# Retention's attention ahead of its gate blocks, single-pass gather and scatter in the expert loop, pairs of experts in two layouts

## The chip, the cores and the metric

The kernel runs on one core of a Trainium2 chip. The metric is the device time of one execution in microseconds (us). Of each version several executions are timed, and the medians are compared. A separate execution is profiled by the hardware; the rows and durations below come from that one.

## What is computed

Two networks run one after the other on 256 tokens of width 1024, all in float32. The first (modulated layers with attention, a Fourier mixer and dense MLPs) is not touched. The second has two layers: each is a mixer followed by a mixture of experts. The mixer of layer 0 is an attention with forget gates ("fox"), that of layer 1 is retention.

```
retention:  q, k, v, gate = split(h @ w_in)                # 1024 -> 6 blocks of 1024 columns: q, k, v0, v1, g0, g1
            q, k = rotary(q), rotary(k) / 16
            o = ((q @ k.T) * decay) @ v                    # 4 heads, 256 tokens
            o = (o - mean(o)) * rsqrt(var(o) + eps) * gn_gain
            y = (silu(gate) * o) @ w_out                   # 2048 -> 1024
experts:    32 experts in 4 groups; each token takes the best group and 2 experts in it
            y[t] = sum over its 2 experts e of gate[t, e] * (silu(x_t @ w_g[e]) * (x_t @ w_u[e])) @ w_down[e]
```

Every expert's weights (w_gu 1024 x 1024, w_down 512 x 1024) are read once a layer.

## The kernel before

Everything is written by hand, engine by engine, with semaphores; the order of the work on an engine is the order of the code. Activations lie transposed (feature on the partition, token on the free axis). SP issues nearly all the loads.

**Dense weights.** A matrix is cut in blocks of 1024 columns, and a block in 4 chunks of 256 rows (1 MB). `dense_w` is a ring of 4 chunks. SP loads a chunk (L461) when PE has done with the one 4 earlier; ACT makes its high part (`w_high`, L428) and DVE the rest (`w_low`, L435), both in the type fp32r, which PE multiplies in one pass. `by_rows` goes through a block chunk by chunk: 8 output tiles, 2 rows of tiles in a chunk, and 3 matmuls for each (high weights x high input, low x high, high x low; L552 to L554). So a block has 192 matmuls of 256 columns. A matmul on plain float32 is one instruction in the code but two records (and two weight loads) in the profile.

**Retention.** PE: blocks q, k, v0, v1, g0, g1 of `ret_in`; the scores of 4 heads (L1058); times v (`ret_pv`, L1070, L1071); the mean over a head's 512 features as a matmul with a constant (`gn_mean`, L582); the variance (`gn_var`); then `keep_warm` (L595), 16 matmuls with constants whose result nobody reads; then the two blocks of `ret_out`. ACT takes the silu of g0 and g1 as they leave PE (L1104), and the square root of the variances (L1116). DVE multiplies scores with the decay (L2207), subtracts the mean (L2212), multiplies gate, value and gain (L2219), and then for each head takes the reciprocal (L1530), multiplies it in (L2226), waits for ACT's high part of the result (L1499) and makes the low one (L1555); only then may PE start a chunk of `ret_out`. `ret_out` has two slots for its high parts (`w_high_ret`), so ACT may split a chunk when PE has done with the one two earlier. On SP, once g1 is done, the 8 loads of the first 4 pieces of the next expert pair come ahead of `ret_out`'s last 4 chunks.

**Experts.** `experts(l)` first turns h into tokens on the partitions (L879), normalises (L1405 on ACT, L1963 on DVE: `hn_tok`), and computes the logits (L886); DVE chooses groups and experts, counts, and gives each row of an expert a place (L1953 to L2087). Then come 16 pairs of experts in a hardware loop. The two experts of a pair share one pass of 128 rows. Per pair PE does: `project` (L945): 8 row tiles x 2 halves, moving the 1024 x 1024 weights of both experts past the gathered rows in column tiles of the array that work at the same time; `gather` (L929) for the next pair: 16 float32 matmuls of 128 columns that pick 128 rows out of `hn_tok` by a 0/1 matrix `pick`; `turn_hidden` (L970), `turn_pick` (L965); `add_up` (L976): 8 float32 matmuls of 256 columns that add the previous pair's output `y_sb` to 4 banks through the transposed weighted matrix `pick_wT`; and `down` (L957). ACT copies the left half of y out of its bank (L1430), DVE the right half (L2102); PE's `pending` waits for both ahead of the next `gather`. The 128 rows are divided 64/64 between the two experts, or 32/96 or 96/32 where both fit that way; three variants of `project` and `down` stand in the code, chosen by a register (L1022, L1038). Where an expert has more rows than its share, a further round is run for the pair.

The weights of a pair are 12 pieces of 1 MB: `load_experts(l, pair, j)` issues two DMAs (L470), one for each expert, j = 0 to 3 for w_gu and 4, 5 for w_down. There is one buffer for each piece: SP issues piece j of the next pair when PE has done with piece j of this one.

## Time and profile before

| | before |
|---|---|
| median of 3 runs | 2210.24 us (2209.28 to 2216.31) |
| the profiled execution's own time | 2208.49 us |
| its span in the profile | 2206.7 us |
| PE busy | 2080.8 us (94%) |
| PE weight loads busy | 1519.7 us (69%) |
| DVE busy | 884.1 us (40%) |
| ACT busy | 687.7 us (31%) |
| moved by DMA | 603.25 MB, mean 273 GB/s |
| PE's share of the chain that ended last | 85% |

The two expert loops run from 953.5 us to 1431.5 us and from 1704.8 us to 2183.0 us of the span; retention lies between 1437 and 1680 us. An engine's busy share is a mean over stages that have different limits; a busy PE is not a PE at its peak, since matmuls overlap. The chain is followed back from the last instruction to whatever released it.

### The profile page before, as it was taken

Reading aid. Unit: us, or ns where it says so; the run is one execution under the profiler, and the core shown is the slowest. Engines: PE = TensorE matmul, PEld = TensorE weight load, DVE = VectorE, ACT = ScalarE, POOL = GpSimd, SP = SyncE. Lnnn points to the kernel's source line nnn. Section 1 sums busy time; section 2 is a strip of 40 time slices with the busy share of each in tenths; the row PEclk is TensorE's granted clock in tenths of the full one; section 3 lists DMA queues with packets and bytes.
Section 4 is the critical chain, followed back from the end, with each engine's and each line's share of the span. In section 5 each row is a group of like instructions: output and inputs, shape, how many; then the busy total and the mean of one; then the engine's idle time right before and its main releaser. Section 6 shows DMA issues by size and latency. Waiting matters only on the chain.

```text
span 2206.7 us, 37943 instructions
## 1 busy us (share of the span) xinstructions
PE 2080.8 (94%) x15688; PEld 1519.7 (69%) x15689; DVE 884.1 (40%) x1459; ACT 687.7 (31%) x1070; POOL 80.3 (4%) x119
## 2 busy tenths in 40 slices
PE   7997899998999998889999999989998999999998
PEld 5876899988999898744544444588987444444454
DVE  5866677755643544521111111156366111111112
ACT  3434455253553456511111111144342111111111
POOL 0110111101000200000000000000000000000000
PEclk9998999999999999989999999989998999999999
DMA  9731388912654251689999999625642899999992
GB/s 360 266 128 39 118 306 320 333 42 77 249 190 175 78 189 39 255 330 422 421 422 422 421 422 422 267 90 189 214 189 98 366 421 421 422 422 422 422 422 123
DMA packets 108115, 603.25 MB, mean 273 GB/s; under 512 B 10078, under 2 KB 10532, under 8 KB 58868
## 3 DMA queue, kind: packets, MB, share of 16 engines
q1 hardware_dynamic: 95872, 559.39, 64.0%
q0 software_dynamic: 11872, 42.35, 5.2%
q8 instruction: 74, 1.21, 0.2%
q14 instruction: 21, 0.17, 0.0%
q10 hardware_dynamic: 276, 0.13, 0.0%
HBM read 600.74 MB, written 1.05 MB: 273 GB/s over the span
## 4 chain that ended last, share of the span: by engine, by line
PE 85%; DVE 5%; ACT 4%; DMA 3%; issue 3%; SPq 0%; DVEq 0%; ACTq 0%
PE bank L945 20%; PE bank L957 10%; PE bank L552 10%; PE bank L553 9%; PE bank L554 9%; PE bank L929 6%; PE bank L976 5%; PE bank L582 4%; DMA dense_w<-in_w_in 1%; PE bank L562 1%; PE bank L563 1%; PE bank L561 1%; PE bank L632 1%; DMA dense_w<-in_mlp_w 1%; ACT w_high L428 1%
## 5 line engine op out<-in xcount | busy, mean ns | idle before, releaser
L945 PE MATMUL bank<-expert_w,work 128*32 128x512 f32 (+1 forms) x4032 | 446.1, 593 | 19.1 <-issue 19.1
L945 PEld LDWEIGHTS bank<-expert_w,work 128*32 128x32 f32 (+1 forms) x4032 | 156.7, 110 | 307.0 <-issue 307.0
L435 DVE TENSOR_TENSOR w_low<-dense_w,w_high 128x2048 fp32r<-128x2048 f32 x112 | 256.1, 2290 | 223.5 <-ACT w_high L428 222.9
L428 ACT ACTIVATE w_high<-dense_w 128x2048 fp32r<-128x2048 f32 x120 | 228.6, 1911 | 313.4 <-DMA dense_w<-in_mlp_w 197.6
L957 PE MATMUL bank<-expert_w,work 128*32 128x512 f32 (+1 forms) x2016 | 226.4, 594 | 0.0
L2092 DVE TENSOR_TENSOR work<-work,bank 128x512 f32<-128x512 f32 x32 | 22.0, 688 | 391.4 <-ACT work L1419 391.4
L929 PEld LDWEIGHTS bank<-work 128*128 128x128 f32 x1088 | 137.3, 205 | 43.9 <-issue 43.9
L957 PEld LDWEIGHTS bank<-expert_w,work 128*32 128x32 f32 (+1 forms) x2016 | 63.6, 110 | 144.4 <-issue 144.4
L929 PE MATMUL bank<-work 128*128 128x128 f32 x1088 | 143.7, 293 | 13.9 <-issue 7.7
L552 PE MATMUL bank<-u_pairs_mlp,w_high 128*128 128x256 f32 x512 | 146.1, 285 | 7.3 <-ACT u_pairs_mlp L1144 5.9
L553 PE MATMUL bank<-u_pairs_mlp,w_low 128*128 128x256 f32 x512 | 145.6, 284 | 0.0
L554 PE MATMUL bank<-u_pairs_mlp,w_high 128*128 128x256 f32 x512 | 145.6, 284 | 0.0
L553 PE MATMUL bank<-hidden_pairs,w_low 128*128 128x256 f32 x512 | 145.1, 283 | 0.0
L554 PE MATMUL bank<-hidden_pairs,w_high 128*128 128x256 f32 x512 | 145.1, 283 | 0.0
L552 PE MATMUL bank<-hidden_pairs,w_high 128*128 128x256 f32 x512 | 145.1, 283 | 0.0
L1419 ACT ACTIVATE work<-bank 128x512 f32<-128x512 f32 x32 | 19.1, 597 | 392.3 <-PE bank L945 392.3
L552 PE MATMUL bank<-u_pairs,w_high 128*128 128x256 f32 x448 | 130.1, 290 | 9.0 <-DVE u_pairs L1537 5.3
L553 PE MATMUL bank<-u_pairs,w_low 128*128 128x256 f32 x448 | 129.0, 288 | 0.0
L554 PE MATMUL bank<-u_pairs,w_high 128*128 128x256 f32 x448 | 128.9, 288 | 0.0
L976 PE MATMUL bank<-work 128*128 128x256 f32 x544 | 123.2, 380 | 1.7 <-ACT work L1430 1.7
L1430 ACT ACTIVATE work<-bank 128x512 f32<-128x512 f32 x32 | 19.1, 597 | 323.5 <-PE bank L957 323.5
L976 PEld LDWEIGHTS bank<-work 128*128 128x128 f32 x544 | 100.8, 190 | 15.7 <-ACT work L1430 3.5
(387 smaller groups left out, 3610.3 us busy)
## 6 DMA issues: line engine op xcount, KB each, us to landing
expert_w<-in_expert_w_gu SPq DMA_DIRECT2D x256, 1024.0 KB, 13.5
expert_w<-in_expert_w_down SPq DMA_DIRECT2D x128, 1024.0 KB, 9.8
dense_w<-in_mlp_w SPq DMA_DIRECT2D x64, 1024.0 KB, 5.3
dense_w<-in_ret_w_in SPq DMA_DIRECT2D x24, 1024.0 KB, 5.3
u<-in_ada_w POOLq DMA_DIRECT2D x40, 512.0 KB, 6.0
work<-in_ada_w POOLq DMA_DIRECT2D x40, 512.0 KB, 7.0
dense_w<-in_fox_w_in SPq DMA_DIRECT2D x16, 1024.0 KB, 5.1
dense_w<-in_w_in SPq DMA_DIRECT2D x12, 1024.0 KB, 7.9
```

Source lines behind the costliest of these rows:

```text
L428: nc.scalar.activation(HIGH_OF[at], dense_w[:, at % RING], ACT.Copy, scale=scale).then_inc(S("w_high_ready"), 1)
L435: ins = nc.vector.tensor_tensor(w_low[:, at % RING], dense_w[:, at % RING], high, ALU.subtract)
L552: mm(out[:, 0:SEQ], w[:, c], high[:, k, :], start=start, stop=False)
L553: mm(out[:, 0:SEQ], w_rest[:, c], high[:, k, :], start=False, stop=False)
L554: return mm(out[:, 0:SEQ], w[:, c], low[:, k, :], start=False, stop=stop)
L561: mm(out[:, :], high[:, k, rows], w[:, c], start=start, stop=False)
L562: mm(out[:, :], high[:, k, rows], w_rest[:, c], start=False, stop=False)
L582: last = mm(bank(t)[:, 0:SEQ], weights, src[:, k, :], start=k == 0, stop=k == tiles - 1)
L929: last = mm(free[2 + half][:, (k % 4) * P:(k % 4 + 1) * P], every_other(hn_tok[:, tt], k), source[:, tt, :], start=tt == 0, stop=tt == TT - 1)
L945: last = mm(free[half][cols, :], rows[:, k, cols], pieces[:, k // 2, a, k % 2, half * 512:(half + 1) * 512], start=k == 0, stop=k == KT - 1)
L957: last = mm(free[2 + half][cols, :], hidT[:, f, cols], pieces[:, (KT + f) // 2, a, f % 2, half * 512:(half + 1) * 512], start=f == 0, stop ...
L976: last = mm(total[k // 2][:, (k % 2) * SEQ:(k % 2 + 1) * SEQ], y_sb[:, k * P:(k + 1) * P], pick_wT.rearrange("p t n -> p (t n)"), start=Fa ...
```

## The change

It has four parts.

1. **Pairs.** The divisions are now 64/64, or 96 rows for the crowded expert and 32 for the other (`LARGE`). Where the second expert of a pair is the crowded one, SP loads the pair swapped: it reads a 0/1 from `more_i` at the head of each turn (a new wait for `more_known` ahead of the loop) and adds it to the address. Pair 0, which is loaded before the counts are known, is not swapped. Of the three variants of `project` and `down` two remain. DVE's arithmetic on the counts is rewritten.
2. **Gather and scatter.** `hn_tok` and `y_sb` become a high and a low part each in fp32r. `gather` has 32 single-pass matmuls of 128 columns in place of 16 float32 ones, `add_up` 16 single-pass ones of 256 columns in place of 8. The matrix for `add_up` is now 0/1 (`pickT`), and the weight of a row is multiplied into y. ACT makes the whole high part (two instructions), DVE the whole low part (two instructions, each after ACT's). The same holds for `hn`: ACT makes 4 high quarters, DVE 4 low ones.
3. **Retention.** PE does scores, values, means and variances right after v1, then g0 and g1, then `ret_out`; `keep_warm` is gone. DVE multiplies gain and reciprocal deviation into the values ahead of the gates. On SP the decay's load moves ahead of 20 loads of `ret_in`, and the loads of the next pair's pieces stand between `ret_out`'s last 4.
4. **A small load.** The gains of the expert norm (8 KB, on POOL's queue) are loaded after 56 of the modulation loads that it stood ahead of.

The core of the diff:

```
@@ TILES
-  ("ret_v1", 4), ("ret_g0", 8), ("ret_g1", 8), ("ret_scores", 4), ("ret_pv", 8), ("gn_mean", 4), ("gn_var", 4),
+  ("ret_v1", 4), ("ret_scores", 4), ("ret_pv", 8), ("gn_mean", 4), ("gn_var", 4), ("ret_g0", 8), ("ret_g1", 8),
@@ SP
+                sp.wait_ge(S(f"more_known_{l}"), 1)
                 with sp.Fori(1, PAIRS) as i:
+                    swap = sp.value_load(more_i[0:1, ds(i + 3 * PAIRS, 1)], min_val=0, max_val=1)
                     for j in range(PIECES // 2):
                         sp.wait_ge(expert_used, PIECES * (PAIRS * l + i - 1) + 2 * j + 2)
-                        load_experts(l, i, j)
+                        load_experts(l, i, j, swap)
...
                     wait_tile(sp, TILES["ret_g1"] + 7)
-                    for j in range(4):
-                        load_experts(1, 0, j)
                     for j in range(RING):
                         load(chunk("ret_out", 1, j))
+                        load_experts(1, 0, j)
@@ PE, experts
                     for k in range(4 * half, 4 * half + 4):
                         for tt in range(TT):
-                            last = mm(free[2 + half][:, (k % 4) * P:(k % 4 + 1) * P], every_other(hn_tok[:, tt], k),
-                                      source[:, tt, :], start=tt == 0, stop=tt == TT - 1)
+                            for x in (hn_high, hn_low):
+                                last = mm(free[2 + half][:, (k % 4) * P:(k % 4 + 1) * P], x[:, tt, k * P:(k + 1) * P], source[:, tt, :],
+                                          start=tt == 0 and x is hn_high, stop=tt == TT - 1 and x is hn_low)
...
                     for k in range(KT):
-                        last = mm(total[k // 2][:, (k % 2) * SEQ:(k % 2 + 1) * SEQ], y_sb[:, k * P:(k + 1) * P],
-                                  pick_wT.rearrange("p t n -> p (t n)"), start=False, stop=False)
+                        for y in (y_high, y_low):
+                            last = mm(total[k // 2][:, (k % 2) * SEQ:(k % 2 + 1) * SEQ], y[:, k * P:(k + 1) * P], pickT,
+                                      start=False, stop=False)
...
-                    for first in SHARES:
+                    for first in (SLOTS, LARGE):
                         with pe.If(first_rows == first):
                             project(xg, loaded, expert_used, first)
@@ PE, retention
-            for i, name in enumerate(("ret_q", "ret_k", "ret_v0", "ret_v1", "ret_g0", "ret_g1")):
+            for i, name in enumerate(("ret_q", "ret_k", "ret_v0", "ret_v1")):
...
-            keep_warm(TILES["ret_out"], 2 * WARM)
+            for i, name in ((4, "ret_g0"), (5, "ret_g1")):
+                by_rows("ret_in", i, TILES[name], 8, columns(*second))
@@ ACT, experts
-                for q in (0, 2):
-                    t = TILES[f"hn_{l}"] + q
-                    evac(fn(hn_tok[:, 0, q // 2 * 512:(q // 2 + 1) * 512], bank(t)[:, :], ACT.Copy, scale=small[:, 88:89]), t)
-                fn(y_sb[:, 0:512], const[:, 0:512], ACT.Copy, scale=0.0).then_inc(S("y_act"), 1)
+                for q in range(4):
+                    fn(hn_part(hn_high, q), bank(TILES[f"hn_{l}"] + q)[:, :], ACT.Copy, scale=small[:, 88 + q % 2:89 + q % 2]).then_inc(S("hn_high"), 1)
...
                 def take_y(done):
-                    fn(y_sb[:, 0:512], free[2][:, :], ACT.Copy).then_inc(done, 1)
+                    for half in range(2):
+                        fn(y_high[:, half * 512:(half + 1) * 512], free[2 + half][:, :], ACT.Copy, scale=slot_w).then_inc(done, 1)
@@ DVE, experts
-                V.memset(y_sb[:, 512:1024], 0.0).then_inc(S("y_dve"), 1)
-                V.memset(pick_wT, 0.0).then_inc(S("pick_wT_ready"), 1)
+                V.tensor_scalar(y_low, const[:, 0:D], 0.0, None, ALU.mult).then_inc(S("y_dve"), 1)
+                V.tensor_scalar(pickT, const[:, 0:SEQ], 0.0, None, ALU.mult).then_inc(S("pick_wT_ready"), 1)
...
+                def low_of_hn(q):
+                    dve.wait_ge(S("hn_high"), 4 * l + q + 1)
+                    evac(V.scalar_tensor_tensor(hn_part(hn_low, q), bank(TILES[f"hn_{l}"] + q)[:, :], small[:, 88 + q % 2:89 + q % 2],
+                                                hn_part(hn_high.bitcast(f32), q), ALU.mult, ALU.subtract), TILES[f"hn_{l}"] + q)
...
                 def take_pick_wT(done):
-                    V.tensor_copy(pick_wT, free[1][:, 0:SEQ].rearrange("p (t n) -> p t n", t=TT)).then_inc(done, 1)
+                    V.tensor_reduce(slot_w, free[1][:, 0:SEQ], AX.X, ALU.add)
+                    V.tensor_scalar(pickT, free[1][:, 0:SEQ], 0.0, None, ALU.is_gt).then_inc(done, 1)
+
+                def take_y(made, at, done):
+                    for half in range(2):
+                        dve.wait_ge(made, at + half + 1)
+                        eight = slice(half * 512, (half + 1) * 512)
+                        last = V.scalar_tensor_tensor(y_low[:, eight], free[2 + half][:, :], slot_w, y_high[:, eight].bitcast(f32),
+                                                      ALU.mult, ALU.subtract)
+                    last.then_inc(done, 1)
@@ DVE, retention
+                inv_std(gn_rstd[:, hd, :], TILES["gn_var"] + hd)
                 for n in range(4 * hd, 4 * hd + 4):
-                    wait_evac(dve, TILES[f"ret_g{n // 8}"] + n % 8)
-                    V.scalar_tensor_tensor(rgate[:, n, :], ro[:, n, :], vcol(VEC1["gn"] + n), rgate[:, n, :],
-                                           ALU.mult, ALU.mult).then_inc(S("ret_gated"), 1)
+                    V.scalar_tensor_tensor(ro[:, n, :], ro[:, n, :], vcol(VEC1["gn"] + n), gn_rstd[:, hd, :],
+                                           ALU.mult, ALU.mult).then_inc(S("ret_scaled"), 1)
```

How the change moves instructions is seen at three places. The first is PE between `project` and `down` in the expert loop (`work` holds the gathered-from tokens, the pick matrices and y). Before:

```order
L1025 REGISTER_ALU
L929 MATMUL bank<-work 128x128 x16
L970 MATMUL bank<-const,work 128x128 x4
L965 MATMUL bank<-const,work 128x128 x2
L976 MATMUL bank<-work 128x256 x8
```

With the change (the first two rows stand 16 times over, as do the last two for 8 row tiles):

```order
L940 MATMUL bank<-pick,hn_high 128x128
L940 MATMUL bank<-pick,hn_low 128x128
L978 MATMUL bank<-const,work 128x128 x4
L973 MATMUL bank<-const,work 128x128 x2
L985 MATMUL bank<-pickT,y_high 128x256
L985 MATMUL bank<-pickT,y_low 128x256
```

The place of the four steps is the same; gather and scatter have twice the instructions, each of a single pass.

The second is DVE from the scores of retention to the residual add after `ret_out`, where PE waits for it. Before:

```order
L2207 TENSOR_TENSOR work<-bank,work 128x384 x4
L2212 TENSOR_TENSOR work<-work,bank 128x1024 x4
L435 TENSOR_TENSOR w_low<-dense_w,w_high_ret 128x2048
L2219 SCALAR_TENSOR_TENSOR work<-work,vec 128x256 x16
L435 TENSOR_TENSOR w_low<-dense_w,w_high_ret 128x2048
L1530 RECIPROCAL work<-work 128x256
L2226 TENSOR_TENSOR work<-work 128x1024
L1555 TENSOR_TENSOR rgate_low<-work,rgate_high 128x256 x4
L1530 RECIPROCAL work<-work 128x256
L2226 TENSOR_TENSOR work<-work 128x1024
L1555 TENSOR_TENSOR rgate_low<-work,rgate_high 128x256 x4
L435 TENSOR_TENSOR w_low<-dense_w,w_high_ret 128x2048 x2
```

With the change (L438 is the low part of a chunk, `w_high` without _ret that of a gate block; L2260 multiplies a gate with its values):

```order
L2251 SCALAR_TENSOR_TENSOR work<-work,vec 128x256 x4
L438 TENSOR_TENSOR w_low<-dense_w,w_high 128x2048 x3
L2260 TENSOR_TENSOR work<-work 128x1024 x2
L438 TENSOR_TENSOR w_low<-dense_w,w_high 128x2048
L1582 TENSOR_TENSOR rgate_low<-work,rgate_high 128x256 x8
L438 TENSOR_TENSOR w_low<-dense_w,w_high_ret 128x2048 x2
L2260 TENSOR_TENSOR work<-work 128x1024 x2
L1582 TENSOR_TENSOR rgate_low<-work,rgate_high 128x256 x8
L438 TENSOR_TENSOR w_low<-dense_w,w_high_ret 128x2048 x6
L1973 TENSOR_TENSOR h<-h,bank 128x256 x8
```

The reciprocals and the gain now stand ahead of the gate blocks' splits, and between a gate block and `ret_out` only one multiplication for a head and the low parts are left.

The third is SP between the two expert loops. Before:

```order
L461 DMA dense_w<-in_ret_w_in 128x2x1024 x20
L509 DMA work<-in_decay 128x1536
L461 DMA dense_w<-in_ret_w_out 128x2x1024 x4
L470 DMA expert_w<-in_expert_w_gu 128x2048 x8
L461 DMA dense_w<-in_ret_w_out 128x2x1024 x4
L470 DMA expert_w<-in_expert_w_down 128x2048 x4
```

With the change (the `ret_out` chunk and the two expert loads behind it stand three times):

```order
L516 DMA work<-in_decay 128x1536
L468 DMA dense_w<-in_ret_w_in 128x2x1024 x20
L468 DMA dense_w<-in_ret_w_out 128x2x1024 x5
L478 DMA expert_w<-in_expert_w_gu 128x2048 x2
L468 DMA dense_w<-in_ret_w_out 128x2x1024
L478 DMA expert_w<-in_expert_w_gu 128x2048 x2
L478 DMA expert_w<-in_expert_w_down 128x2048 x4
```

Each of the last chunks of `ret_out` but the first has the two loads of an expert piece ahead of it.

## Rows read from the trace of the kernel before

**Rows 1.** The page's slices: busy tenths of PE and DMA, each slice 55 us
```profile
PE   7997899998999998889999999989998999999998
...
DMA  9731388912654251689999999625642899999992
```

**Rows 2.** Window over layer 1's expert loop: length, busy by engine, clock, DMA share, GB/s
```profile
1740.00:2160.00 420.00, 412.69 (x3504) 202.55 (x3500) 73.54 (x217) 60.27 (x113) 0.00 (x0) 1.00 1.01 422
```

**Rows 3.** Chain of waits, expert loops: start us, us, what
```profile
1225.58 13.96 PE bank L945 x64
...
1402.39 13.94 PE bank L945 x128
...
1718.72 3.67 issue
...
2124.26 13.94 PE bank L945 x128
2138.20 3.97 PE bank L929 x32
2142.86 3.46 PE bank L976 x16
...
2153.83 13.94 PE bank L945 x128
...
2182.95 0.61 ACT work L1430
2183.74 3.69 PE bank L976 x16
```

**Rows 4.** Line L470, piece 3 of pair 2, layer 1: issue and landing
```profile
L470 SPq DMA_DIRECT2D expert_w<-in_expert_w_gu x2: 332/332/333, 1753.9 to 1754.4; - x2
...
DMA to landing us min/median/max: 12.9/13.8/14.8
```

**Rows 5.** The same of pair 15, layer 1
```profile
L470 SPq DMA_DIRECT2D expert_w<-in_expert_w_gu x2: 333/333/333, 2138.4 to 2138.9; - x2
...
DMA to landing us min/median/max: 16.3/17.3/18.3
```

**Rows 6.** The same of pair 15, layer 0
```profile
L470 SPq DMA_DIRECT2D expert_w<-in_expert_w_gu x2: 332/332/333, 1387.0 to 1387.5; - x2
...
DMA to landing us min/median/max: 17.2/18.2/19.1
```

**Rows 7.** SP's timeline: the first loads of pair 1's w_down, layer 1
```profile
1735.79 4.28 SPq L470 DMA_DIRECT2D expert_w<-in_expert_w_down  x4
```

**Rows 8.** Windows: block g1, keep_warm, behind it, ret_out's start, layer 1's first gather
```profile
1622.30:1629.40 7.10, 7.08 (x33) 5.90 (x31) 7.07 (x11) 0.47 (x1) 0.00 (x0) 1.00 0.00 0
1629.40:1631.80 2.40, 0.00 (x0) 0.01 (x1) 1.92 (x4) 1.29 (x4) 0.00 (x0) 1.00 0.00 0
1631.80:1637.00 5.20, 5.18 (x43) 5.20 (x44) 4.68 (x8) 1.39 (x5) 0.00 (x0) 1.00 0.00 0
...
1697.00:1703.20 6.20, 6.13 (x32) 5.95 (x32) 1.72 (x11) 2.31 (x5) 0.00 (x0) 0.62 0.02 4
...
1570.00:1592.90 22.90, 22.90 (x193) 22.90 (x192) 4.59 (x2) 6.71 (x10) 0.00 (x0) 1.00 0.60 219
```

**Rows 9.** PE's timeline in ret_out: the wait in brackets
```profile
1656.38 0.39 PE L552 MATMUL bank<-rgate_high,w_high_ret 128*128 128x256 f32 x1 [1.29 <-DVE w_low L435]
```

**Rows 10.** DVE's timeline ahead of layer 1's logits
```profile
1683.71 1.41 DVE L1963 TENSOR_SCALAR work<-bank,small 128x512 f32<-128x512 f32 x2
```

**Rows 11.** The page's groups and issues: splits of a chunk, DVE on a bank, a chunk's load
```profile
L435 DVE TENSOR_TENSOR w_low<-dense_w,w_high 128x2048 fp32r<-128x2048 f32 x112 | 256.1, 2290 | 223.5 <-ACT w_high L428 222.9
...
L2092 DVE TENSOR_TENSOR work<-work,bank 128x512 f32<-128x512 f32 x32 | 22.0, 688 | 391.4 <-ACT work L1419 391.4
...
dense_w<-in_ret_w_in SPq DMA_DIRECT2D x24, 1024.0 KB, 5.3
```

**Rows 12.** Chain of waits: float32 records of 256 columns while the clock is low
```profile
1439.69 6.70 PE bank L582 x16
```

247 lines of the change are left out of this document (139 added, 108 removed).

## The prediction, made before the changed kernel ran

> **What bounds the kernel now.** The page's slices come first: PE is busy nearly everywhere, and in the two expert loops the DMA engines are full as well [rows 1]. A window over layer 1's loop says it sharply: DMA share 1.01 at 422 GB/s for 420 us, PE busy 413 of 420 at full clock, ACT and DVE mostly idle [rows 2]. Two full resources need a third view, the chain of waits. It shows a pair of experts as PE's work alone: project 13.94 us, gather 3.97, add_up 3.46, then down; and from one project to the next 2153.83 - 2124.26 = 29.57 us [rows 3]. No step waits for a load. But a pair's 12 MB are 12.58 million bytes, and at 422 GB/s they take 29.8 us, 0.26 us longer than PE. So the loads must lose ground, and the landings show it: piece 3 of pair 2 in layer 1 landed 14.8 us after its issue, at 1754.4 + 14.8 = 1769.2 [rows 4]; that of pair 15 took 18.3 us and landed at 2157.2 [rows 5]. PE first needs piece 3 three quarters into project, 10.46 us after its start: at 2164.3 for pair 15. It had 7.1 us to spare. In layer 0 it landed at 1387.5 + 19.1 = 1406.6 and was needed at 1402.39 + 10.46 = 1412.85: 6.2 us to spare [rows 3, 6]. **PE bounds the loops, with DMA just below it**: a faster PE wins about that reserve once a layer, and no more.
>
> Retention is PE's alone, with three losses: 7.1 us of matmuls with constants, 2.4 us of idleness behind them, while DVE and ACT finish the first head, and 1.29 us in ret_out [rows 8, 9].
>
> **Expert loops.** add_up has 16 single-pass matmuls of 256 columns in place of 16 float32 records. In block g1 such matmuls follow each other every 22.9 / 193 = 0.119 us [rows 8], so it takes 1.9 us in place of 3.46: 1.5 less. gather has 32 single-pass matmuls of 128 columns, a form that the trace does not show. From below: half the price of the 256-column form, 0.06 us, 1.9 us in all. From above: the price of a float32 record of 256 columns, 3.46 / 16 = 0.216 us, 6.9 us in all. The nearest rows agree with each other: float32 records of 128 columns come every 3.97 / 32 = 0.124 us, single-pass ones of 256 every 0.119 [rows 3, 8], and both load 128 x 128 weights for each matmul, which fills PEld in g1 (22.90 of 22.90 us). I take 0.119, 3.8 us in all, 0.1 less than before. PE's pair becomes 28.0 us, less than the 29.8 of its loads.
>
> The Trainium skill's page TensorE: Matmul & The Clock Gate (Back-to-back issue gap) gives about 81 ns for a matmul of 128 columns in a stream with its weight loads. By that estimate gather would take 2.6 us; the sum would be some 5 us lower, from the first and last pair of each layer, since between them the loads bound. No row here shows it.
>
> So the reserve is used up at 1.9 us a pair: by about pair 7 PE waits for piece 3, some 1.8 us each time. What moves the end: SP issues pair 1's first w_down piece when pair 0 has used its own, at 1735.79 in layer 1 [rows 7], and from there on DMA never rests. A shorter pair 0 brings this and all later landings forward by 1.6 us. Piece 3 of pair 15 lands at 2157.2 - 1.6 = 2155.6; the last quarter of project is 3.5 us; from there to the end of down were 2182.95 - 2153.83 - 13.94 = 15.2 us and are 13.6 [rows 3]. The loop ends at 2172.7 in place of 2182.95: **-10.2 us**. Layer 0 in the same way: 1406.6 - 1.6 + 3.5 = 1408.5 in place of 1416.3, and 1.6 behind it: **-9.4 us**. The 3.67 us of issue after pair 0's first project [rows 3] I leave as it is; with other code it may be 0 or double, which moves each layer by up to 4 us either way.
>
> Would waits of 1.8 us lower the clock? Behind the warming PE idled 2.40 us, and the granted clock stayed 1.00 in the windows on both sides [rows 8]. I charge nothing.
>
> Behind the loop, y's chain was 0.79 us from the last matmul to add_up. Now ACT makes one half (0.61), DVE its low part (0.69, as on another whole bank), ACT's second half lies beside this, and DVE's second follows: with hand-offs 2.2 us, 1.4 more; add_up saves 1.7 of its 3.69 [rows 3, 11]. **-0.3 a layer.** Inside the loop the same chain, and one more DVE pass over the pick matrix, have 13.9 us of project as their cover. Without it the chain would cost its 2.2 us a pair.
>
> **Pairs and variants.** The pair with two tiles of 64 columns took 13.96 us for project, those with four of 32 took 13.94 [rows 3]: fewer instructions, no time. Worked out from the reference's inputs, pair 0 holds 1 and 4 rows in layer 0 and 10 and 7 in layer 1, and every crowded expert (at most 78 rows) shares with one of at most 29 or counts under 65, so no pair gets a further round; one would cost a whole pass, near 29 us. SP's register read lies between w_down's issues and the next expert_used, and SP's queue has a reserve of microseconds there: nothing. Its new wait ahead of the loop ends before PE's first project, which frees the first piece.
>
> **Routing.** ACT's first high quarter (0.61) now precedes DVE's two low ones (2 x 0.69) where both engines worked at once for 1.41 [rows 10, 11]: +0.8. Zeroing 1024 elements by arithmetic in place of a MEMSET of 512 adds 0.3 (bounds: nothing, and the 0.7 of another instruction on 512). The two later low quarters fall in DVE's wait for PE's counts; the counts' own chain is two or three small steps shorter, -0.2. **+0.9 a layer.** The first gather is as slow as before (6.13 us for 32 records at a mean clock of 0.62).
>
> **Retention.** The six blocks and the statistics keep their length; ret_out follows g1 directly. Gone are 7.1 + 2.4 + 1.3: **-10.8 us**. The cover: values' statistics, reciprocals and gains are DVE work under g0's 23 us; g0's silu, product and parts lie under g1; g1's lie under ret_out's first block. If that cover fails, the first product, high and low part cost some 5 us. The last chunks of ret_out now queue behind 2 MB of expert weights: 2.1 million bytes at 422 GB/s are 5.0 us, then 5.3 for the chunk, somewhat less than DVE on ACT (say 1.9), and 2.3 on DVE, together 14.5, against three chunks of 5.7 (22.9 / 4) that PE has in between [rows 8, 11]. The decay's load waits ahead of loads that could not start anyway. The 8 KB load saves or costs nothing that a wait shows.
>
> **Sum.** -10.8 - 10.2 - 9.4 - 0.6 + 1.8 = -29.2 us. The profiled execution took 2208.5 us, so 2179.3; the median of the runs is 1.7 higher, so **2181 us**. A measurement of this kernel tells from no change what exceeds 0.3%, 6.6 us.
>
> **Rivals.**
> - *Gather turns slow (slower).* If a single-pass matmul of only 128 columns costs as much as a float32 record of 256, gather takes 6.9 us, a pair 29.57 + 2.9 - 1.5 = 31.0: PE bounds again, 16 x 1.4 = 22 us more a layer. At the low clock of the first gather such records take 6.70 / 16 = 0.42 us [rows 12], so that one takes 13.4 in place of 6.1. Together 59 - 0.6 - 10.8 + 1.8 = +50: 2260 us. It decides from 0.18 us a matmul, where the loops lose what retention gains. For it: the form is nowhere in the trace. Against it: no form that is there is bound by anything but columns and weight loads. 0.16.
> - *Retention wins nothing.* The removed idleness comes back as waits for splits or evacuations, since ACT splits two gate chunks ahead of the values' evacuation: 2192 us. The arithmetic above speaks against it. 0.10.
> - *The loops win little*: waits for loads cost clock or restart the queue late, so that the 20 us fall away: 2201 us. Rows 8 speak against the clock, and six pieces in flight against a dry queue. 0.08.
> - *Loads run faster.* Now PE bounds the loops, and perhaps 422 GB/s is its pace and not DMA's. Then 16 x 1.6 a layer are won, 2150 us. The growing landing times contradict it [rows 4, 5]. 0.04. The Trainium skill's page DMA: Bandwidth & Descriptors (Where 436 GB/s comes from) puts the fabric's ceiling at 435 GB/s, an estimate of 28.9 us a pair, which would give most of this; the trace's 422 stands against it.
>
> **Numbers.** The forecast has the other 0.62. Its own bounds are 2172 (gather at its lower price, 1.9 us less in the first and last pair of each layer, and a shorter stall) to 2192. Taking in the second and third rival the range is 2172 to 2204, which leaves out 0.20. Faster: 0.62 + 0.10 + 0.04 + 0.03 of the third rival = 0.79; within 0.3%: 0.05; slower: 0.16.
>
> **What would show it.** In the changed profile: PE from v1 to ret_out without a gap, no constant matmuls; pairs about 29.8 us apart in the later half of each loop, at DMA share 1.01, with waits before the last quarter of project whose releaser is the expert load; the first pairs 28.0 us apart; gather near 3.8 and add_up near 1.9 us. A gather over 5.8 us, or pairs over 30 us apart, would make the prediction wrong; so would loops with no wait for a load.

## The result, and the profile after

| | before | after |
|---|---|---|
| median of the runs shown | 2209.76 us (4 runs, 2200.74 to 2216.31) | 2230.72 us (4 runs, 2224.55 to 2235.49) |
| ratio, 95% interval | | 1.0096 [1.0049, 1.0143] |
| the profiled execution | 2208.49, span 2206.7 | 2224.55, span 2222.7 |

The change made the kernel 1% slower, about 21 us; forecast were 2181 us and a range that ended at 2204. The stretches of the two profiled executions say where (a loop runs from the first `project` of a layer to its last `down`):

| | before | after | difference | forecast |
|---|---|---|---|---|
| start of layer 0's loop | 953.5 | 949.3 | -4.2 | +0.9 |
| loop of layer 0 | 478.0 | 523.1 | **+45.1** | -9.4 |
| between the loops (with retention) | 273.3 | 263.3 | -10.0 | -10.2 |
| loop of layer 1 | 478.1 | 465.0 | -13.1 | -10.2 |
| behind it | 23.8 | 22.1 | -1.7 | -0.3 |

Three of the five came out within 3 us of the forecast. The start of layer 0's loop is 5 us off, which is at least in part scatter (late_gains, below). One is off by 55 us, and in one layer only. The page of the changed kernel shows the place in its slices, which answer to [rows 1] (each slice is 55.6 us):

```profile
PE   7997899998999998899999999989999999999997
...
DMA  9731389803645251789998957935447699999994
GB/s 347 268 133 40 141 305 331 316 35 114 229 177 184 78 189 52 292 367 422 422 422 369 374 227 295 422 128 171 133 142 313 258 422 422 422 422 422 422 422 206
```

PE looks busy as before, but in layer 0's loop (slices 18 to 27) DMA falls from 422 to 227 GB/s; in layer 1's it doesn't. The chain of waits in layer 0 has the cause, in three pairs of 16 (8, 10 and 11, counted from 0):

```profile
1167.49 7.02 PE bank L965 x32
1174.51 31.61 PE bank L953 x96
1206.12 3.72 PE bank L940 x32
...
1210.61 1.91 PE bank L985 x16
1212.52 15.88 PE bank L965 x48
1228.39 13.88 PE bank L953 x64
```

x64 is a pair in two tiles of 64 columns, x96 one of the new division 96/32 in three tiles, of 64, 32 and 32 columns. Its `project` takes 31.6 us and not 13.9, its `down` 15.9 and not 7.0: 26.7 us more. PE's weight loads in the same `project` say how (columns: start, time, and in brackets the idle time before):

```profile
1181.25 0.14 PEld L953 LDWEIGHTS bank<-expert_w,work 128*32 128x32 f32 x4 [0.81 <-issue]
1182.23 0.19 PEld L953 LDWEIGHTS bank<-expert_w,work 128*64 128x64 f32 x2 [0.84 <-issue]
1183.23 0.14 PEld L953 LDWEIGHTS bank<-expert_w,work 128*32 128x32 f32 x4 [0.81 <-issue]
```

The 64-column tile and the two 32-column ones take turns, 0.99 us each; two tiles of one width share 0.86 us (13.73 / 16). The three tiles cost two turns where four equal tiles cost one.

Layer 1 has no 96/32 pair, and there the forecast can be read step by step. Its chain, which answers to [rows 3]:

```profile
1735.60 16.63 PE bank L953 x64
1752.23 3.72 PE bank L940 x32
...
1756.72 1.90 PE bank L985 x16
...
1765.64 13.73 PE bank L953 x64
...
1792.79 13.73 PE bank L953 x64
...
2128.24 25.34 DMA expert_w<-in_expert_w_gu
2153.59 0.14 issue
2153.72 3.67 PE bank L953 x16
...
2158.06 25.35 DMA expert_w<-in_expert_w_gu
2183.42 0.14 issue
2183.55 3.65 PE bank L953 x16
```

Gather takes 3.72 us (forecast 3.8) and add_up 1.9 (1.9). Behind pair 0 the pairs are 27.1 us apart at first (1792.79 - 1765.64; forecast 28.0); from pair 6 on they are 29.83 apart (2183.42 - 2153.59), and the last quarter of `project` (x16) is released by the load of piece 3, as forecast. PE's busy time in the window that answers to [rows 2] fell from 412.7 to 399.1 us:

```profile
1740.00:2160.00 420.00, 399.08 (x2180) 191.99 (x2177) 87.39 (x239) 69.74 (x130) 0.00 (x0) 1.00 1.00 418
```

Retention: windows over g0's and g1's end, then `ret_out`, which answer to [rows 8, 9], show PE without a gap:

```profile
1618.04:1664.00 45.96, 45.96 (x385) 45.96 (x385) 29.43 (x32) 20.82 (x31) 0.00 (x0) 1.00 0.48 161
1664.00:1710.18 46.18, 46.18 (x387) 46.18 (x387) 20.70 (x22) 15.94 (x17) 0.00 (x0) 1.00 0.74 296
```

### The profile page after: what moved, and what is told of

It is laid out like the page before. It is cut to its first block, busy times and chain, and to the rows that moved or that the text cites. A ratio compares the mean times of both kernels' runs of the same rounds, so it can differ in the third digit from the quotient of the medians.

```text
span 2222.7 us, 32423 instructions
## 1 busy us (share of the span) xinstructions
PE 2093.5 (94%) x12824; PEld 1473.4 (66%) x12825; DVE 919.7 (41%) x1529; ACT 713.5 (32%) x1108; POOL 80.5 (4%) x119
## 4 chain that ended last, share of the span: by engine, by line
PE 72%; DMA 17%; DVE 4%; ACT 4%; issue 2%; SPq 0%; ACTq 0%; DVEq 0%
PE bank L953 16%; DMA expert_w<-in_expert_w_gu 16%; PE bank L561 10%; PE bank L562 10%; PE bank L563 10%; PE bank L965 7%; PE bank L591 4%; PE bank L940 4%; PE bank L985 2%; PE bank L571 1%; PE bank L570 1%; PE bank L572 1%; PE bank L641 1%; DMA dense_w<-in_w_in 1%; DVE work L1557 1%
## 5 line engine op out<-in xcount | busy, mean ns | idle before, releaser
L953 PE MATMUL bank<-expert_w,work 128*64 128x512 f32 (+1 forms) x2144 | 508.8, 600 | 31.9 <-DMA expert_w<-in_expert_w_gu 28.3
L953 PEld LDWEIGHTS bank<-expert_w,work 128*64 128x64 f32 (+1 forms) x2144 | 154.1, 135 | 380.4 <-issue 380.4
L438 DVE TENSOR_TENSOR w_low<-dense_w,w_high 128x2048 fp32r<-128x2048 f32 x112 | 256.0, 2290 | 213.3 <-ACT w_high L431 212.5
L965 PE MATMUL bank<-expert_w,work 128*64 128x512 f32 (+1 forms) x1072 | 253.4, 597 | 0.0
L965 PEld LDWEIGHTS bank<-expert_w,work 128*64 128x64 f32 (+1 forms) x1072 | 72.1, 134 | 157.3 <-issue 153.0
L1429 ACT ACTIVATE work<-bank 128x512 f32<-128x512 f32 x32 | 19.1, 598 | 457.9 <-PE bank L953 457.9
L2133 DVE SCALAR_TENSOR_TENSOR y_low<-bank,small,y_high 128x512 fp32r<-128x512 f32 x64 | 45.1, 746 | 252.9 <-ACT y_high L1441 252.9
L1441 ACT ACTIVATE y_high<-bank,small 128x512 fp32r<-128x512 f32 x64 | 40.6, 685 | 302.9 <-PE bank L965 302.9
L940 PE MATMUL bank<-pick,hn_high 128*128 128x128 f32 x544 | 128.3, 282 | 4.1 <-DVE pick L2090 4.1
L940 PEld LDWEIGHTS bank<-pick,hn_high 128*128 128x128 f32 x544 | 106.7, 196 | 33.1 <-issue 33.1
L940 PE MATMUL bank<-pick,hn_low 128*128 128x128 f32 x544 | 126.9, 280 | 0.0
```

What stands on the lines that cost most here:

```text
L438: ins = nc.vector.tensor_tensor(w_low[:, at % RING], dense_w[:, at % RING], high, ALU.subtract)
L940: last = mm(free[2 + half][:, (k % 4) * P:(k % 4 + 1) * P], x[:, tt, k * P:(k + 1) * P], source[:, tt, :], start=tt == 0 and x is hn_high, ...
L953: last = mm(free[half][cols, :], rows[:, k, cols], pieces[:, k // 2, a, k % 2, half * 512:(half + 1) * 512], start=k == 0, stop=k == KT - 1)
L965: last = mm(free[2 + half][cols, :], hidT[:, f, cols], pieces[:, (KT + f) // 2, a, f % 2, half * 512:(half + 1) * 512], start=f == 0, stop ...
L1441: fn(y_high[:, half * 512:(half + 1) * 512], free[2 + half][:, :], ACT.Copy, scale=slot_w).then_inc(done, 1)
L2133: last = V.scalar_tensor_tensor(y_low[:, eight], free[2 + half][:, :], slot_w, y_high[:, eight].bitcast(f32), ALU.mult, ALU.subtract)
```

## The experiments

Each ratio is to the kernel before, run on the same chip in the same rounds. Widths are in columns.

### Is it the widths of the tiles?

**four_tiles.** The changed kernel, one line changed:

```
-                            LARGE: [(slice(0, SLOTS), 0), (slice(SLOTS, LARGE), 0), (slice(LARGE, P), 1)]}
+                            LARGE: [(slice(at, at + UNIT), int(at >= LARGE)) for at in range(0, P, UNIT)]}
```

> The changed kernel with the 96/32 division as four tiles of 32 columns, as the kernel before had it. Theory (a tile of 64 columns does not work at the same time as tiles of 32): project of the three 96/32 pairs falls from 31.6 to 13.9 us and down from 15.9 to 7.0; waits for loads of about 2 us a pair appear instead, as in layer 1; the loop of layer 0 falls from 523 to about 465 us, and the kernel's median from 2231 to about 2172 (2165 to 2180), 1.5% or more below the kernel before. Rival (the swapped address makes these pairs' loads or the reading of their weights slow): project of these pairs stays at 31.6 and the time at 2231. Rival (the second variant's code is fetched slowly): project stays well above 20 us.

Measured: 2175.39 us, ratio 0.9841 [0.982, 0.9862]. The loops take 465.0 and 465.1 us. The three pairs wait for their loads like the others. Its chain:

```profile
1188.91 3.68 PE bank L953 x32
1193.25 25.37 DMA expert_w<-in_expert_w_gu
1218.75 3.67 PE bank L953 x16
```

x32 is the last quarter of a 96/32 pair in four tiles, x16 that of a 64/64 pair. The window over these pairs is full of loads again:

```profile
1255.00:1363.00 108.00, 100.83 (x675) 49.14 (x675) 24.09 (x67) 18.14 (x33) 0.00 (x0) 1.00 1.01 422
```

One line is worth 55 us (2230.7 to 2175.4; the spans differ by 53.7). The swapped address and the choice between two variants still stand in this kernel, so they are not the cause, and it is faster than the kernel before and the changed one.

**grouped.** Three tiles again; within each k both matmuls of the 64-column tile come first:

```
+                    return [(half, tile) for wide in (True, False) for half in range(2) for tile in tiles_of[first]
+                            if (tile[0] == slice(0, SLOTS)) == wide]
```

> Still tiles of 64, 32 and 32 columns, but for each row tile the two matmuls of the 64-column tile (left and right half) stand together, and then the four of the 32-column tiles: two changes of width for a row tile in place of four. Theory, with a price of 0.13 us for each change of width (0.988 us for a stretch of one width in place of 0.855): project 8 x (4 x 0.855 + 2 x 0.13) = 29.4 us in place of 31.6, down 14.7 in place of 15.9; kernel about 2222. Rival (no price for the change, each matmul of such a set is only slow): both stay at 31.6 and 15.9, kernel 2231.

Measured (one execution): `project` 29.46 us, `down` 14.81, kernel 2213 us, its loop in layer 0 513.7 us in place of 523.1. Its weight loads:

```profile
1180.88 0.14 PEld L959 LDWEIGHTS bank<-expert_w,work 128*64 128x64 f32 x1 [0.29 <-issue]
1181.31 0.14 PEld L959 LDWEIGHTS bank<-expert_w,work 128*64 128x64 f32 x1 [0.29 <-issue]
1182.26 0.14 PEld L959 LDWEIGHTS bank<-expert_w,work 128*32 128x32 f32 x4 [0.81 <-issue]
1182.72 0.12 PEld L959 LDWEIGHTS bank<-expert_w,work 128*32 128x32 f32 x2 [0.31 <-issue]
```

While the width stays, the next weights are loaded 0.29 us after the last ones (0.31 for 32 columns), beside the running matmul. Where it changes, they wait 0.81 us, until the matmuls in the array have all but ended: the last one began at 1181.74 and is given 0.59 us, the load starts at 1182.26. So there are two prices: tiles of unlike width share no time (0.855 us a matmul), and a change of width costs 0.13 us on top. The first is most of it.

**wide_between.** The order of the three tiles is 32, 64, 32:

```
-                            LARGE: [(slice(0, SLOTS), 0), (slice(SLOTS, LARGE), 0), (slice(LARGE, P), 1)]}
+                            LARGE: [(slice(SLOTS, LARGE), 0), (slice(0, SLOTS), 0), (slice(LARGE, P), 1)]}
```

> The same three tiles, but the 64-column one stands between the two of 32, so that no two tiles of one width follow each other in a set. Theory (only neighbours of equal width work at the same time): of a set and the next, 32, 64, 32 and again 32, 64, 32: the last 32 and the first 32 of the next set are of one width but the latter uses other columns, so they may pair up; then a set costs 0.988 x 2 as before and project stays at 31.6 us. If both go one after the other, a set costs about 2.8 us and project about 45, down 22.7, kernel about 2290. Rival (a set with unequal widths costs what it does by its widths, whatever the order): 31.6.

Measured (one execution): 2228 us.

```profile
1174.62 32.73 PE bank L953 x96
...
1213.74 16.85 PE bank L965 x48
```

It is one turn more than 31.61, 1.1 us: the last 32-column tile of a set pairs up with the first of the next, and only the first and the last of all stand alone. What counts is whether neighbours in the stream have one width, not how a set is made up.

**before_three.** The kernel before, with the three tiles alone:

```
-                    return [(slice(at, at + UNIT), int(at >= first)) for at in range(0, P, UNIT)]
+                    if first > SLOTS:
+                        return [(slice(0, SLOTS), 0), (slice(SLOTS, first), 0), (slice(first, P), 1)]
+                    return [(slice(0, UNIT), 0), (slice(UNIT, SLOTS), 1), (slice(SLOTS, P), 1)]
```

> The kernel before, with nothing of the change but the tiles: wherever it divides 96/32 or 32/96, tiles of 64, 32 and 32 columns take the place of four of 32. It does so in 15 of 16 pairs of layer 0 and, by its trace, in all pairs seen of layer 1. Theory: project 31.6 in place of 13.9 and down 15.9 in place of 7.0 in each, some 26.6 us a pair less the nothing that loads gave, so about 31 x 26.6 = 820 us more: 3030 us. Rival (the cost belongs to the swap, the second variant or another part of the change): 2210 us.

Measured (one execution): 3007 us, 796 more. Without any other part of the change:

```profile
1008.90 31.76 PE bank L947 x96
...
1048.77 15.88 PE bank L959 x48
```

### Where do the loops win?

With this out of the way, each loop gains 13 us. The forecast gave such a gain to the single passes.

**no_add_up.** Left out: the sum of 15 of 16 pairs of each layer.

```
-                    add_up().then_inc(S("added"), 1)
+                    mm(total[0][:, 0:SEQ], y_high[:, 0:P], pickT, start=False, stop=False).then_inc(S("added"), 1)
```

> The kernel with four tiles, where one matmul stands in the loop for the sixteen that add a pair's output: 15 of 16 pairs of a layer are left out of the sum. Theory (the loads bound the loops): PE has 1.8 us less a pair, only the first and the last pair of each layer give it back, 4 x 1.8 = 7 us: 2168; pairs late in the loop still 29.8 us apart. Rival (PE and its waits bound, the loads follow): 32 x 1.8 = 57 us less, 2118.

Measured: 2162.6 us, ratio 0.9785 [0.9752, 0.9819], 12.8 below four_tiles where 7 were expected, and far from 57. In layer 1 pairs start 26.1 us apart and from pair 5 on 29.8: the loads bound the loop. By the profiles its loops are only 0.1 and 2.1 us shorter. The profiled execution is the slowest of its four and four_tiles' the fastest of its five; the rest of the 12.8 I can't place.

**float_gather.** four_tiles, with gather and add_up in float32 again:

```
-                            for x in (hn_high, hn_low):
-                                last = mm(free[2 + half][:, (k % 4) * P:(k % 4 + 1) * P], x[:, tt, k * P:(k + 1) * P], source[:, tt, :],
-                                          start=tt == 0 and x is hn_high, stop=tt == TT - 1 and x is hn_low)
+                            last = mm(free[2 + half][:, (k % 4) * P:(k % 4 + 1) * P], hn_high.bitcast(f32)[:, tt, k * P:(k + 1) * P],
+                                      source.bitcast(f32)[:, tt, :], start=tt == 0, stop=tt == TT - 1)
```

> The kernel with four tiles, with the tokens and y kept whole in float32 and gather and add_up as 16 and 8 float32 matmuls again, as before the change; the low parts are still made but not read. Theory (the prediction's term for the single passes: they bring PE's pair from 29.6 to 28 us, and the loads keep what is beyond 0.26 us a pair): gather 3.97 and add_up 3.46 us return, a pair takes 29.6 us of PE and 29.8 of loads, no wait for a load is left but near the end, and each loop is longer by what pair 0, the last pair and the used-up reserve are worth, 9 to 10 us: 2194. Rival (a loop bound by loads takes what its loads take, whatever PE does): within 3 us of the kernel with four tiles.

**four_again** is four_tiles on the same chip.

> The kernel with four tiles once more, beside the next two on one chip, so that they can be compared with it directly. By its first runs 0.984 of the kernel before, 2175 us.

Measured: 2175.03 us for float_gather, ratio 0.9858 [0.983, 0.9885], against 2172.15 us, 0.9835 [0.9809, 0.9861]. The rival holds: 3 us by the medians and 5 by the ratios, whose intervals overlap, in place of some 20. Its pairs in layer 1:

```profile
1706.55 13.73 PE bank L952 x64
1720.29 3.77 PE bank L939 x32
...
1724.75 3.46 PE bank L983 x16
1728.20 7.02 PE bank L964 x32
1735.22 13.73 PE bank L952 x64
```

A pair takes 28.67 us and not the 29.6 that I expected. 0.2 us of this is gather: its 32 float32 records take 3.77 us where they took 3.97 before, and they do so with four tiles too (float_all_four, below), so the tiles are not the reason. It now reads its weights from adjacent columns and no longer from every other one; that this is the reason no run shows by itself. The rest, 0.7 us, lies almost all between `down` and the next `project`: no idle time is left there, where four 32-column tiles before had 0.5, and the first matmuls of `project` begin before the last of `down` have ended. From its start to gather's `project` itself takes 13.83 us against 13.87. Fifteen times 0.9 is 13 us, twice the reserve of 7. So the loads bind these loops too, if later (from pair 10 on).

**all_four_tiles** and **float_all_four.** four_tiles and float_gather, with 64/64 in four tiles too:

```
-                tiles_of = {SLOTS: [(slice(0, SLOTS), 0), (slice(SLOTS, P), 1)],
+                tiles_of = {SLOTS: [(slice(at, at + UNIT), int(at >= SLOTS)) for at in range(0, P, UNIT)],
```

> The kernel with four tiles, where the 64/64 division too has four tiles of 32 columns in place of two of 64, as most pairs of the kernel before had; single-pass gather and add_up stay. Theory (a pair of two 64-column tiles is 0.2 us shorter in project and has none of the 0.5 us between down and the next project, and either this or the single passes alone is enough to use up the reserve of the loads): pairs of 27.9 us until the loads bind, each loop still about 465 us, kernel within 3 us of the one with four tiles only for 96/32 (2172 to 2175). Rival (the tiles are what shortened the loops): loops of 476 to 478 us, about 2195.

> Both at once: float32 gather and add_up, and four tiles of 32 columns for every division. Theory: the pair is 29.6 us as before the change, nothing uses up the reserve, each loop is 10 to 12 us longer again (475 to 478 us), the kernel 2193 to 2198. Rival (what is saved comes from the number of variants, or from pair 0 alone): loops of 466 to 470 us, 2175 to 2180.

Measured, with ratio to the kernel before, early pairs and loops:

| gather, add_up | 64/64 in | median us | ratio | early pairs us | loop 0, loop 1 us |
|---|---|---|---|---|---|
| single passes | two tiles | 2172.15 | 0.9835 | 27.1 | 470.1, 464.7 |
| float32 | two tiles | 2175.03 | 0.9858 | 28.7 | 467.8, 465.8 |
| single passes | four tiles | 2181.84 | 0.9882 | 27.6 | 464.1, 473.2 |
| float32 | four tiles | 2196.24 | 0.994 | 29.1 | 467.6, 475.9 |

The first two rows ran side by side on one chip, the last two on another. Against the last row, by the ratios, the single passes alone win 0.0058 (12.8 us), the tiles alone 0.0082 (18.1), both together 0.0105 (23.2) and not 30.9. Each ratio is uncertain by 0.002 to 0.003, so that this shortfall alone shows little. My two expectations missed in part: all_four_tiles is 10 us above four_again, not 3, and float_all_four's first loop did not return to 475.

Where the differences lie is seen when the loops of the profiled executions are divided at the second `project` (all in us, layer 0 and layer 1):

| | idle ahead of the first project | first pair | other 15 pairs |
|---|---|---|---|
| kernel before | 1.8, 1.6 | 35.3, 35.0 | 442.6, 443.1 |
| single passes, two tiles | 1.8, 1.7 | 34.6, 29.2 | 435.6, 435.5 |
| float32, two tiles | 1.8, 1.8 | 31.0, 28.7 | 436.8, 437.0 |
| single passes, four tiles | 5.3, 4.9 | 29.9, 38.5 | 434.1, 434.8 |
| float32, four tiles | 5.7, 4.6 | 31.2, 39.0 | 436.4, 437.0 |

Behind the first pair the four are within 3 us of each other, and each is 6 to 9 us below the kernel before. Even the last, which has neither the single passes nor the wide tiles, wins 6.2 us a layer there: its pairs start 29.1 us apart and not 29.6, since gather takes 3.77 us in place of 3.97 and the idle time behind `down` is shorter:

```profile
1361.70 0.24 issue
1361.95 13.94 PE bank L952 x128
```

Between `down` and the next `project` PE idles 0.24 us where the kernel before, with its three variants, idled 0.50. In layer 0 the first pair adds 4.1 us to this (35.3 to 31.2), which brings that loop to 467.6. Fifteen times the 0.46 by which the pairs are nearer are 6.9 us, about the whole reserve, and the last two `project`s of layer 1 already take 14.1 and 14.2 us in place of 13.9. So what is common to all four kernels nearly uses the reserve up; the single passes add 1 to 2 us behind the first pair, the tiles nothing.

The tiles' 18 us are elsewhere. Of the 21.9 us between the spans of the two float32 kernels 10.2 are the first pair of layer 1, and 4.0 and 2.9 are idle time ahead of the two first `project`s. That pair in all_four_tiles' timeline of PE:

```profile
1684.62 1.92 PE L953 MATMUL bank<-expert_w,work 128*32 128x512 f32 x5 [4.91 <-issue]
1687.53 15.86 PE L953 MATMUL bank<-expert_w,work 128*32 128x512 f32 x123 [0.99 <-issue]
1706.09 0.30 PE L940 MATMUL bank<-pick,hn_high 128*128 128x128 f32 x1 [2.70 <-issue]
```

It lasts 38.5 us. Ahead of it and within it lie 4.9 + 1.0 + 2.7 us in which PE waits for nothing that the profile shows, and behind the 2.7 the granted clock fell: from 1706.0 to 1715.5 its mean was 0.64, and gather and add_up took 5.8 and 3.6 us from start to start in place of 4.3 and 2.1.

First pairs also differ between executions of one kernel: in layer 0 that of four_tiles took 31.0 us and that of four_again 34.6, since the clock fell in the second behind 2.5 us of idle time (0.50 from 970 to 975 us) and not in the first behind 1.9.

### What is the idle time in the first pair?

**three_variants.** four_tiles, with a third variant that no pair takes:

```
-                    for first in (SLOTS, LARGE):
+                    for first in (UNIT, SLOTS, LARGE):
```

> The kernel with four tiles, and with the third variant of project and down (32/96) back in the code, where no pair takes it. Theory (the idle time of PE behind the first project of a layer, 4.04 and 3.67 us before and 1.91 and 0 now, is fetching of the code that stands between): it grows back to about 4 us in both layers, pair 0 is that much longer, and the loops, bound by loads that start with pair 0, end about 2 to 4 us later each: 2179 to 2183 against 2175.4. Rival (the gap comes from something else, and code that is not run costs nothing): 2175.4.

Measured: 2182.15 us, ratio 0.9885 [0.9857, 0.9912], 7 us above four_tiles by the medians, 10 by the ratios. The place is not the one that I named: the gap grew ahead of the first project, where the variant that is skipped stands.

```profile
1680.87 7.79 issue
```

In four_tiles it was 1.73 us there; in layer 0, 5.19 against 1.76. Together that is 9.5 us of the 9.3 between the two profiled executions, and the loops themselves are as long as in four_tiles (464.8 and 464.9 us). In all_four_tiles too, where these gaps are 5.3 and 4.9 us, there is more code to skip ahead of the first project: the further round, which no pair takes, has four tiles there. The profile's DMA queue of instructions points the same way (packets, MB, share):

```profile
q8 instruction: 74, 1.21, 0.2%
```

It has 74 packets here and in the kernel before, 73 in the two runs with four tiles for both divisions, 71 and 70 in four_tiles and four_again, 70 in the changed kernel, and 80 in retention_only, below.

The Trainium skill's page Runtime: NRT & Kernel Launch (Terms) says that each engine's instruction memory is refilled in blocks of 16 KB; 1.21 MB in 74 packets is 16.4 KB each, which agrees. That PE waited for such a block in the gaps is argued from this and from the places of the gaps; no row names a releaser.

The idle time between `down` and the next `project` follows the number of variants too: between two 96/32 pairs it was 0.23 us in four_tiles and 0.63 here, like the 0.24 of float_all_four and the 0.50 of the kernel before.

### Retention and the small load

**retention_only.** The kernel before, with part 3 of the change alone (the retention part of the diff above, on all engines; its core):

```
-            keep_warm(TILES["ret_out"], 2 * WARM)
+            for i, name in ((4, "ret_g0"), (5, "ret_g1")):
+                by_rows("ret_in", i, TILES[name], 8, columns(*second))
```

> The kernel before with the change's retention alone: scores, values and norm ahead of the gate blocks, no matmuls with constants, the decay's load early, the last weights between expert pieces. Theory (the prediction's term): 7.1 + 2.4 + 1.3 = 10.8 us less, 2199.8 against a median of 2210.6; the stretch between the end of layer 0's experts and the first sum of layer 1's routing is 10.8 shorter. Rival (nothing won): 2210.6, with new waits of PE for splits of the gate blocks or of the output weights.

Measured: 2199.24 us, ratio 0.9965 [0.9944, 0.9986], 8 us of its runs' 2207.3 (3 to 12). In its profile retention, from the first layer's last add_up (1445.15) to the first sum of layer 1's routing (1676.44), takes 231.3 us against 244.2 before, 12.9 less. But the same execution loses as much in the loop of layer 0, in whose second and third turn, too, gaps appear that the kernel before had in the first alone:

```profile
1003.09 6.61 PE L928 MATMUL bank<-work 128*128 128x128 f32 x32 [3.99 <-issue]
1021.37 13.94 PE L944 MATMUL bank<-expert_w,work 128*32 128x512 f32 x128 [0.53 <-issue]
```

The code of that loop and all PE code ahead of it are those of the kernel before, word for word; what differs stands behind the loop. So the change does not explain these gaps, no wait that the profile shows does either, and their cause stays open. The profiled execution, 2208.78 us, is the second slowest of twelve, which scatter from 2192 to 2215 us.

**old_retention.** four_tiles with retention as before the change (the same edit, backwards).

> The kernel with four tiles with the retention of the kernel before: gate blocks ahead of the scores, matmuls with constants ahead of the output weights. Theory: 10.8 to 12.9 us longer than the kernel with four tiles (10.8 is the prediction's term, 12.9 what the stretch between the loops showed with retention alone). Rival (the median of retention alone, 8 us, is the true size): 8 us.

Measured: 2187.27 us, ratio 0.9904 [0.9879, 0.9929], 15.1 above four_again; the stretch between the loops is 273.7 us against 259.9, 13.8 more. From the last add_up to the first sum of routing, as measured above, it is 243.8 against 231.0, 12.8 more; in the changed kernel it is 232.3 us, 11.8 less than before. By the profiles, then, retention is worth 11.8 to 12.9 us.

**late_gains.** The kernel before, with the 8 KB load moved:

```
-            pool.dma_start(ffn_gain[:, :].rearrange("p (k r) -> p k r", r=2),
...
                     load_ada(pool, q)
+            pool.dma_start(ffn_gain[:, :].rearrange("p (k r) -> p k r", r=2),
```

> The kernel before with nothing of the change but the 8 KB load of gains moved behind the 56 modulation loads. The prediction's term: nothing. Rival (that load of 1024 packets of 8 bytes holds up POOL's queue and the modulation loads behind it, and the wait of 7.06 us for the last of them at 434 us is its effect): the wait goes and the first expert loop starts 3 to 5 us earlier, 2206 us.

Measured: 2208.71 us, ratio 1.0007 [0.9982, 1.0033]: nothing, as forecast. The first sum of layer 0's routing, at 928.3 us before and 923.3 in the changed kernel, came between 921.8 and 927.1 in the twelve profiled executions with this load moved, and at 928.3, 924.8 and 927.9 in the three without. A gain of 2 or 3 us is neither shown nor excluded; the 4.2 us at the start of the changed kernel's loop are at least in part scatter.

## Why the prediction was wrong

**The step that failed** is "Pairs and variants", where I wrote: "The pair with two tiles of 64 columns took 13.96 us for project, those with four of 32 took 13.94: fewer instructions, no time." Both rows hold tiles of one width. The changed layout has 64, 32 and 32, which stood in no row, and I took it for something between the two that did. Gather, also a form that the trace did not show, had bounds and a rival; this had neither. By my own rows a bound from above was at hand: if tiles of unlike width share no time, a set costs two turns of 0.87, 13.9 us more for `project` and 7 for `down`; with the change of width on top it was 26.7 a pair. Three such pairs make 3 x (54.0 - 29.8) = 73 us, and five pairs behind or between them run at 27.1 in place of 29.8, since the loads catch up meanwhile: 73 - 14 = 59 us, against 58.1 between the two loops (523.1 and 465.0). I had even counted the rows of each expert, enough to know how many pairs would be divided 96/32.

The Trainium skill's page TensorEngine Tiling (Array Packing), section Key Properties, says: "Changing tiling mode (not just tile) drains the TensorE", and lists 128 rows by 64 and 128 rows by 32 columns as modes apart. The runs agree, and add the price: 0.13 us a change, and with it the 0.86 us a turn that tiles of unlike width no longer share.

**The same step was wrong a second time, the other way.** Two tiles of 64 do take less than four of 32, if not in `project` (13.83 us against 13.87 to gather's start): it is the idle time behind `down`. The trace of before showed it: its one 64/64 pair [rows 3] began at 1225.58 and the next at 1254.59, 29.0 us later and not 29.6; on the way in, the pair ahead of it had lost 0.25. I compared durations of `project` and not starts. And leaving out the third variant, which stood in the sum at nothing, saves 0.26 us of idle time a pair.

**The loops came out near the forecast for another reason than mine.** I gave the gain of each loop to the single passes. In layer 1 it is 13.1 us: 5.1 in the first pair and 8.0 behind it. Of the 8.0, float_all_four wins 6.2 without them. That -13.1 stands beside -10.2 is therefore in part luck: the bound by the loads was right, and with the reserve so small nearly any saving on PE reaches it.

**What held.** *The bound of the loops*: pairs 29.83 us apart (forecast 29.8), released by piece 3, DMA at 422 GB/s, and next to no help from a PE with less work. *Gather and add_up*: 3.72 us, by the nearest rows and not the lower 2.6, and 1.9. *The reserve* was used up in pair 5 and not about pair 7, PE's pair being 27.1 us and not 28.0. *Pair 0's shift* was 5.1 us in layer 1 and 6.5 in layer 0, not 1.6. In layer 1 the 3.67 us of issue behind the first project went, and so did the low clock of the gather behind them (1.4 us); against it, that project began at a clock of 0.50 and took 16.6 us in place of 13.9. My bound of 4 us either way for these gaps covers layer 1 and not layer 0. *The clock* stayed at 1.00 in the loop's window, waits or not. *Retention*: -11.8 to -12.9 us against -10.8, without a stall; the queue of weights behind 2 MB of experts held up nothing. *Routing*: from its first sum to the first project 25.17 us became 25.96 in layer 0, +0.8 against +0.9, and +0.3 in layer 1. *y's chain* took 2.3 us in both layers, as forecast (2.2); in layer 1 it and add_up took 4.5 us together as before, in layer 0 1.4 more, since add_up ran at a lower clock there (below). With the layout of four tiles, the only one that it had a row for, the sum gave 2181; that kernel takes 2172 to 2175, with the terms of pair 0 and of the time a pair takes on PE off in its favour.

**The rivals.** None of them had this mechanism; "gather turns slow" was the only slower one, and gather was fast.

## What to carry to other kernels

A form of instruction that the trace doesn't show has no price between two that it does; bound it from both sides, even where an edit looks like tidying. In a stream of column tiles give neighbours one width: four tiles of 32 beat 64 + 32 + 32 by more than a factor of two. Where savings draw on one reserve, take them all out before naming which one pays, and divide the loop at its first turn: here neither of the two that I had in mind was needed.

## What the runs showed of the hardware

- Tiles of unlike width take turns (0.99 us each, for float32 matmuls of 512 columns), and the next weights are loaded only when the matmuls ahead have all but ended: 0.81 us after the last load, 0.29 where the width stays.
- Code that isn't run has a price: a third variant of two steps in a loop cost 3.4 and 6.1 us ahead of the loop's first turn in the two layers (one profiled execution; the medians differ by 7 us), and about 0.3 us between two turns with four tiles.
- One execution had idle time of 4 us in the second and third turn of a loop, and the low clock behind it, 12.7 us in all, though the code of the loop and ahead of it was unchanged. Its cause is open.
- 32 single-pass matmuls of 128 columns follow each other every 0.116 us (3.72 / 32); the 32 records of 16 float32 ones took 3.77 to 3.97 us: nearly the same time.
- The same idle time of 2.3 us ahead of the last add_up left the granted clock at 1.00 in layer 1 and not in layer 0, where 16 matmuls took 3.65 us in place of 2.15; in both PE had been busy at full clock for over 10 us:

```profile
1474.70:1478.30 3.60, 3.60 (x18) 3.60 (x18) 0.00 (x0) 0.00 (x0) 0.00 (x0) 0.53 0.00 0
2203.00:2205.00 2.00, 2.00 (x18) 2.00 (x18) 0.00 (x0) 0.00 (x0) 0.00 (x0) 1.00 0.00 0
```

0.53 of full speed is near the lower of its two levels, 1.2 GHz, so I can't tell from the length of a gap alone what it will cost.
